# Low parts of the recurrence outputs moved from VectorE to GpSimd, and a new order at the seam between recurrence and attention, in a hybrid decoder block

## The chip, the cores and the metric

The kernel runs on one core of one Trainium2 chip. The metric is the device time of one execution in microseconds; the time of the kernel before is the median of three runs.

## What is computed

One decoder block on 512 tokens plus 16 prepended meta tokens, width 1024, all in float32. The reference, cut to the parts that matter here:

```python
y = _rmsnorm(h, mix_norm_g[l])
z = y @ w_in[l]
hq, hf, hi, hgate, aq, ak, av, ga, gb = jnp.split(z, offsets, axis=-1)
o_hg = _hgrn2(hq, hf, hi, lbs[l])                      # recurrence, 4 heads of 128
o_hg = _rmsnorm(o_hg, hg_norm_g[l]).reshape(B, L, 512) * jax.nn.silu(hgate)
o_at = _swa_sinks(aq, ak, av, attn_sinks[l])           # window attention, 8 query heads, 2 kv heads
g_hg, g_at = sigmoid(ga + b), sigmoid(gb + b)
m = g_hg * (o_hg @ w_branch_hg[l]) + g_at * (o_at @ w_branch_attn[l])
h = h + m @ w_out[l]
h = h + _peer(_rmsnorm(h, ffn_norm_g[l]), ...)         # product-key experts, 16384 rows of u and v
out = _rmsnorm(h, final_norm_g)[:, N_META:]
```

(Shapes and reshapes are shortened here.) The expert part at the end is by far the longest.

## The kernel before

**Split products.** Every large product is made in three passes on TensorE. A float32 tensor x is held as `hi`, a rounded copy, and `lo` = x - `hi`, and x·w is hi·hi + lo·hi + hi·lo (`SPLIT`). ScalarE makes the `hi` parts (a copy into the rounded type) and GpSimd or VectorE the `lo` parts (a subtraction). The weights come as a stream of tiles of 128 x 1024: SyncE loads one of two raw buffers, ScalarE makes `wzhi` (`split_hi`, line 728), GpSimd `wzlo` (`spread_lo`, line 578), and TensorE then runs 24 products of 512 columns with the tile.

**No scheduler.** Each engine has one instruction stream written out by hand; engines meet at semaphores only. What stands behind a waiting instruction on the same engine waits too.

**The stage of the change.** After the projections come the recurrence (four token tiles, `tt` = 0 to 3) and the attention (steps `i` = 0 to 16, one pair of heads and a token tile of 128 in each). Both are chains of small operations, so TensorE fills its time between them with the 384 products of the 16 gate tiles (`gate_products`, line 1806): 24 before the recurrence, 24 in each `tt`, 8 at the seam (`GATES_MID`) and 15 or 16 in each attention step. Behind each gate tile t:

- ScalarE runs `gate_out(t)` when its 24 products are done: it copies the result out of PSUM (line 790) and makes the `hi` part of weight tile t + 2 (line 728), whose buffer tile t has freed.
- GpSimd then makes the `lo` part of tile t + 2 (line 578) and multiplies gate row t by the row norm (`scale_block`, line 589).
- TensorE needs the `lo` part of tile t + 2 before its first product (`w_lo` in `gate_products`).

**Where `gate_out` stands on ScalarE.** In attention step i, gate tiles finished in the first `GATES_SOON` products of the step come at the step's end; those finished later in it come in the next step:

```python
if i:
    for t in gate_blocks_done(gates_before(i - 1) + GATES_SOON, gates_before(i)):
        gate_out(t)
...
for t in gate_blocks_done(gates_before(i), gates_before(i) + GATES_SOON):
    gate_out(t)
```

**An attention step.** TensorE: transposes of step i - 1 (`turn`, line 1922 and 1923), half of the gate products, `scores(i + 1)`, the other half, and after every fourth step `values` (lines 1932 and 1938). VectorE: `logits(i)` (lines 1330, 1333), then, when ScalarE's exponentials (line 856) are there, `normalise(i)`: a reciprocal (line 1340), two scalings of `atp` by a column (line 1343), and a small product into `atpm` (line 1344), whose end releases `turn(i)`. `queries_lo` (line 1282) makes low parts of later queries in six of the steps.

**The recurrence outputs.** For each `tt` ScalarE takes sums of squares (`o_sq`, line 837) and a root (line 841), VectorE scales (`natural`, line 1265, into `o_nat`), TensorE transposes (`turn_outputs`, line 1866), VectorE multiplies with the output gate into `o_hg` (`gated`, line 1274). For the last `tt` this happens at the seam, inside attention step 0. Later ScalarE makes `ohg["hi"]` of one head in steps 2, 4, 6 and 8 (line 899), and VectorE makes `ohg["lo"]` in steps 3, 7, 11 and 14 (`HG_LO`, line 1377). The branch products after the attention need all of them.

Of the kernel before, what the change touches and what calls it, by code (L numbers as in the profile page):

```python
# [118 lines left out]
HD_AT = 2  # L119
QUERY_HI = {3: 2, 7: 3}  # L120
QUERY_LO = {1: (1, 0), 2: (1, 1), 4: (2, 0), 6: (2, 1), 8: (3, 0), 10: (3, 1)}
HG_LO = (3, 7, 11, 14)
GATES_SOON = 8
QUARTERS = 4
SPAN = LEN // 2
XSUM_AT = 6
# [77 lines left out]
def build(nc, xT, x, params, sinks, ffn_g, final_g, wstream, uT, u, v, gates_dram, acc_dram, out):  # L204
    ctx = ExitStack()
    with ctx:
# [340 lines left out]
        def _(pool):  # L547
# [66 lines left out]
                pool.tensor_tensor(key_lo[s][:], key_raw[:, s], key_hi[:, s].bitcast(F32), ALU.subtract  # L614
                                   ).then_inc(S["key_ok"], 1)

            for t in range(2):
                spread_lo(T_GATE + t + 2, t % 2)
                scale_block(gates[:, t:t + 1], "gate_copied", t + 1, "gate_out")
                keys_lo(t)  # L620
            scale_blocks(T_GATE + 2, T_BRANCH - 2, gates, T_GATE, "gate_copied", "gate_out")
            for t in range(N_GATE - 2, N_GATE):
                split_lo(T_GATE + t + 2, t % 2, slot(t % 2))
                scale_block(gates[:, t:t + 1], "gate_copied", t + 1, "gate_out")
# [92 lines left out]
        def _(act):  # L717
# [113 lines left out]
            act.wait_ge(S["z_out"], N_Z)  # L831
            act.activation(osig[:], og_z, ACT.Sigmoid).then_inc(S["og_sig"], 1)
            for tt in range(TT):
                act.wait_ge(S["o_mm"], (tt + 1) * P // CH)
                for r in range(PER):
                    c = tt * PER + r
                    act.activation(o_sq[:, r, :], ps[:, tt % 2, r * P:(r + 1) * P], ACT.Square,
                                   accum_out=o_stat[:, 0, c:c + 1]).then_inc(S["o_sum"], 1)
                own = slice(tt * PER, (tt + 1) * PER)
                act.wait_ge(S["o_sum"], (tt + 1) * PER)  # L840
                act.activation(o_stat[:, 1, own], o_stat[:, 0, own], ACT.Sqrt, bias=eps[:], scale=1.0 / P
                               ).then_inc(S["osd_ok"], 1)
                for t in gate_blocks_done(GATES_TURN + tt * GATES_HG, GATES_TURN + (tt + 1) * GATES_HG):
                    gate_out(t)
                if tt == TT - 2:
                    act.wait_ge(S["wsc_mm"], TT)
                    queries_hi(0)
                    queries_hi(1)
# [291 lines left out]
        def _(dve):  # L1140
# [221 lines left out]
            for i in range(HEADS):  # L1362
                logits(i)
                if i == 0:
                    natural(TT - 1)
                    gated(TT - 1)
                if i and i % 4 == 0:
                    meta_lo(i // 4 - 1)
                normalise(i)
                if i in QUERY_LO:  # L1370
                    queries_lo(*QUERY_LO[i])
                if i >= 5 and i % 4 == 1:
                    attention_lo(i // 4 - 1)
                if i in HG_LO:
                    h = HG_LO.index(i)
                    dve.wait_ge(S["ohg_hi"], h + 1)
                    dve.tensor_tensor(ohg["lo"][:, h, :], o_hg[:, h, :], ohg["hi"][:, h, :].bitcast(F32),
                                      ALU.subtract).then_inc(S["ohg_ok"], 1)
            meta_lo(TT - 1)
            attention_lo(TT - 1)  # L1380

# [319 lines left out]
        def _(pe):  # L1701
# [205 lines left out]
            pe.wait_ge(S["z_out"], N_Z)  # L1907
            scores(0)
            gate_products(GATES_TURN + TT * GATES_HG, GATES_TURN + TT * GATES_HG + GATES_MID)
            turn_outputs(TT - 1)  # L1910

            def turn(p):

                tt, c = p // 4, p % 4
# [26 lines left out]
            for i in range(HEADS + 1):  # L1941
                if i:
                    turn(i - 1)
                first, last = gates_before(i), gates_before(i + 1)
                gate_products(first, (first + last) // 2)
                if i + 1 < HEADS:
                    scores(i + 1)
                gate_products((first + last) // 2, last)
                if i and i % 4 == 0:
                    values(i // 4 - 1)  # L1950
# [373 lines left out]
```

## Time and profile before

| | |
|---|---|
| median of 3 runs | 1558.53 us (1558.51 to 1559.04) |
| profiled execution | 1558.55 us, its span 1556.7 us |
| TensorE matmul | 1548.4 us busy, 99% of the span |
| VectorE | 1280.5 us, 82% |
| GpSimd | 753.8 us, 48% |
| ScalarE | 695.4 us, 45% |
| granted TensorE clock | 1.0 of full speed over the whole span |

The span runs from the first to the last instruction; 1.85 us of the time lie outside it. Recurrence and attention, the stage of the change, lie between 130 and 262.6 us. A busy TensorE in this table can still lose time, since matmuls overlap in the pipeline: inside the stage it is better read from the distance between starts, which is 0.23 us for gate products that follow one another.

### The profile page before, as it was taken

Reading aid. Unit: us, or ns where it says so; the run is one execution under the profiler, and the core shown is the slowest. Engines: PE = TensorE matmul, PEld = TensorE weight load, DVE = VectorE, ACT = ScalarE, POOL = GpSimd, SP = SyncE. Lnnn points to the kernel's source line nnn. Section 1 sums busy time; section 2 is a strip of 40 time slices with the busy share of each in tenths; the row PEclk is TensorE's granted clock in tenths of the full one; section 3 lists DMA queues with packets and bytes.
Section 4 is the critical chain, followed back from the end, with each engine's and each line's share of the span. In section 5 each row is a group of like instructions: output and inputs, shape, how many; then the busy total and the mean of one; then the engine's idle time right before and its main releaser. Section 6 shows DMA issues by size and latency. Waiting matters only on the chain.

```text
span 1556.7 us, 25687 instructions
## 1 busy us (share of the span) xinstructions
PE 1548.4 (99%) x9433; PEld 1377.6 (88%) x9433; DVE 1280.5 (82%) x2548; ACT 695.4 (45%) x1012; POOL 753.8 (48%) x484
## 2 busy tenths in 40 slices
PE   9999999999999999999999999999999999999998
PEld 9987777888889999999989899999999999888887
DVE  5898665836899899999588787888888888888887
ACT  6333566444343477777433333333333333333334
POOL 4675345434566566654255455555545455322220
PEclk9999999999999999999999999999999999999999
DMA  4322122433224489998899999998999989988984
GB/s 163 97 95 75 63 68 89 142 123 135 81 85 146 142 276 320 322 326 264 311 369 359 338 343 344 341 352 337 347 345 341 358 328 333 328 302 318 334 319 147
DMA packets 151730, 385.44 MB, mean 248 GB/s; under 512 B 11872, under 2 KB 61536, under 8 KB 151520
## 3 DMA queue, kind: packets, MB, share of 16 engines
q1 hardware_dynamic: 59328, 203.13, 36.3%
q0 software_dynamic: 41472, 151.01, 27.1%
q10 hardware_dynamic: 50848, 30.30, 6.7%
q8 instruction: 40, 0.66, 0.2%
q14 instruction: 42, 0.34, 0.1%
HBM read 355.03 MB, written 28.84 MB: 247 GB/s over the span
## 4 chain that ended last, share of the span: by engine, by line
PE 83%; DVE 10%; issue 5%; POOL 2%; ACT 1%; ACTq 0%; POOLq 0%
PE ps L2221 32%; PE ps L2064 26%; PE ps L1743 6%; PE ps L2082 5%; PE ps L1970 3%; DVE hot_w L1627 3%; DVE rows L1566 3%; PE ps L1806 1%; PE ps L1983 1%; DVE hot_l L1623 1%; DVE hot_l L1628 1%; DVE hot_l L1624 1%; PE ps L2207 1%; PE ps L2145 1%; PE ps L1751 1%
## 5 line engine op out<-in xcount | busy, mean ns | idle before, releaser
L2064 PE MATMUL ps<-hThi,uwhi 128*128 128x352 f32 x1024 | 330.1, 326 | 0.0
L2064 PE MATMUL ps<-hTlo,uwhi 128*128 128x352 f32 x1024 | 327.7, 322 | 0.0
L1017 ACT ACTIVATE vwhi<-vraw 128x1024 fp32r<-128x1024 f32 x128 | 135.8, 1061 | 408.0 <-PE ps L2221 353.7
L686 POOL DMA_INDIRECT rows<-in_v,gidx x128 | 163.2, 1275 | 251.3 <-DVE acc L1582 235.1
L686 POOL DMA_INDIRECT rows<-in_u,gidx x128 | 189.2, 1478 | 182.3 <-DVE rows L1575 138.5
L1541 DVE TENSOR_TENSOR vwlo<-vraw,vwhi 128x1024 fp32r<-128x1024 f32 x128 | 156.6, 1223 | 112.3 <-ACT vwhi L1017 112.1
L971 ACT ACTIVATE uwhi<-uraw 128x1024 fp32r<-128x1024 f32 x127 | 134.3, 1058 | 168.8 <-PE ps L2064 133.4
L2064 PEld LDWEIGHTS ps<-hTlo,uwhi 128*128 128x128 f32 x1024 | 192.6, 188 | 1.6
L2064 PEld LDWEIGHTS ps<-hThi,uwhi 128*128 128x128 f32 x1024 | 192.2, 188 | 1.9 <-issue 0.3
L2064 PE MATMUL ps<-hThi,uwlo 128*128 128x352 f32 x1024 | 183.8, 322 | 0.0
L2221 PE MATMUL ps<-vwhi,awhi 128*128 128x512 f32 x720 | 183.7, 390 | 0.0
L2221 PE MATMUL ps<-vwlo,awhi 128*128 128x512 f32 x720 | 182.7, 389 | 0.0
L2221 PE MATMUL ps<-vwhi,awlo 128*128 128x512 f32 x720 | 182.7, 389 | 0.0
L646 POOL TENSOR_TENSOR uwlo<-uraw,uwhi 128x1024 fp32r<-128x1024 f32 x52 | 125.4, 2411 | 96.7 <-ACT uwhi L971 63.2
L1582 DVE SCALAR_TENSOR_TENSOR acc<-rows,pick_w,acc 128x1024 f32<-128x1024 f32 x128 | 164.4, 1284 | 4.2 <-DMA rows<-in_v,gidx 1.7
L2064 PEld LDWEIGHTS ps<-hThi,uwlo 128*128 128x128 f32 x1024 | 166.7, 188 | 0.0
L2221 PEld LDWEIGHTS ps<-vwlo,awhi 128*128 128x128 f32 x720 | 135.1, 188 | 28.3
L2221 PEld LDWEIGHTS ps<-vwhi,awlo 128*128 128x128 f32 x720 | 135.2, 188 | 28.1
L1575 DVE SCALAR_TENSOR_TENSOR rows<-rows,ynat 128x1024 f32<-128x1024 f32 x128 | 154.8, 1231 | 6.1 <-DMA rows<-in_u,gidx 6.0
L2221 PEld LDWEIGHTS ps<-vwhi,awhi 128*128 128x128 f32 x720 | 134.0, 188 | 25.7
L578 POOL TENSOR_TENSOR wzlo<-raw,wzhi 128x1024 fp32r<-128x1024 f32 x35 | 86.3, 2467 | 110.4 <-ACT wzhi L728 110.3
L1058 ACT ACTIVATE piece<-ps 128x512 f32<-128x512 f32 x96 | 100.9, 1168 | 16.0 <-PE ps L2145 16.0
(382 smaller groups left out, 2959.3 us busy)
## 6 DMA issues: line engine op xcount, KB each, us to landing
vraw<-in_v SPq DMA_DIRECT2D x128, 512.0 KB, 5.4
uraw<-in_uT SPq DMA_DIRECT2D x127, 512.0 KB, 5.1
raw<-in_wstream SPq DMA_DIRECT2D x70, 512.0 KB, 3.5
gmat<-gates_dram SPq DMA_DIRECT2D x64, 384.0 KB
gates_dram<-piece ACTq DMA_DIRECT2D x11, 2048.0 KB, 14.4
xt<-in_xT SPq DMA_DIRECT2D x8, 264.0 KB, 4.9
acc<-in_x ACTq DMA_DIRECT2D x4, 512.0 KB, 4.5
rows<-in_u,gidx POOLq DMA_INDIRECT x128, 7.3
```

The source lines that it names most:

```text
L578: pool.tensor_tensor(spaced(k, "lo"), loaded(k), spaced(k, "hi").bitcast(F32), ALU.subtract).then_inc(S["w_lo"], 1)
L646: pool.tensor_tensor(u_weights("lo", n, False), uraw[:, n % 2, :], u_weights("hi", n, False).bitcast(F32), ALU.subtract).then_inc(S["u_lo" ...
L686: pool.indirect_dma_start(out=rows[n % SLOTS][:], out_offset=None, in_=u if q < P else v, in_offset=bass.IndirectOffsetOnAxis(ap=gidx[:, q ...
L971: act.activation(u_weights("hi", n, n >= LAG), u_raw(n, k), ACT.Copy).then_inc(S["u_hi"], 1)
L1017: act.activation(vw["hi"][:, m % 2, :], vraw[:, m % 2, :], ACT.Copy).then_inc(S["v_hi"], 1)
L1058: act.activation(piece[o % 2][:, :, t:t + 4].rearrange("p i t -> p t i"), ps[:, 4 + batch % 2 * 2 + q, :].rearrange("p (t i) -> p t i", t= ...
L1541: dve.tensor_tensor(vw["lo"][:, m % 2, :], vraw[:, m % 2, :], vw["hi"][:, m % 2, :].bitcast(F32), ALU.subtract).then_inc(S["v_lo"], 1)
L1575: dve.scalar_tensor_tensor(out=row[:], in0=row[:], scalar=1.0, in1=ynat[:, 0, :], op0=ALU.mult, op1=ALU.mult, accum_out=dots[:, k:k + 1]). ...
L1582: dve.scalar_tensor_tensor(out=acc[:, 0, :], in0=row[:], scalar=pick_w[:, k:k + 1], in1=acc[:, 0, :], op0=ALU.mult, op1=ALU.add).then_inc( ...
L1743: ins = pe.matmul(dst, z_weights(k, a, c), y[b][:, SLOT[c], own], start=i == 0, stop=i == 3 * DC - 1)
L2064: ins = pe.matmul(ps[:, k, 0:UCOLS], u_weights(a, k, far)[:, c * P:(c + 1) * P], hT[b][:, c, P + EXTRA:TOK], start=i == 0, stop=i == len(U ...
L2221: ins = pe.matmul(ps[:, 2 + j, :], act_w[a][:, k, j // 2 * P:(j // 2 + 1) * P], vw[b][:, k, j % 2 * 512:(j % 2 + 1) * 512], start=first an ...
```

## The change

1. `ohg["lo"]` is made by GpSimd, head h right behind `scale_block` of gate tile 7 + h; VectorE no longer makes it. GpSimd's loop over gate tiles is written out for this.
2. `GATES_SOON` goes from 8 to 11. Of the 16 gate tiles this moves `gate_out(6)` from step 3 to the end of step 2, and `gate_out(11)` from step 11 to the end of step 10.
3. At the seam: ScalarE runs `gate_out(4)` ahead of the last sums of squares instead of behind the root; VectorE runs the last `gated` behind `normalise(0)` instead of ahead of it; TensorE runs the last `turn_outputs` behind `scores(1)`, 7 gate products and one pair of score products later.

```diff
-HG_LO = (3, 7, 11, 14)
-GATES_SOON = 8
+HG_LO = (7, 8, 9, 10)
+GATES_SOON = 11
...
-            for t in range(2):
+            for t in range(N_GATE - 2):
                 spread_lo(T_GATE + t + 2, t % 2)
                 scale_block(gates[:, t:t + 1], "gate_copied", t + 1, "gate_out")
-                keys_lo(t)
-            scale_blocks(T_GATE + 2, T_BRANCH - 2, gates, T_GATE, "gate_copied", "gate_out")
+                if t < 2:
+                    keys_lo(t)
+                if t in HG_LO:
+                    h = HG_LO.index(t)
+                    pool.wait_ge(S["ohg_hi"], h + 1)
+                    pool.tensor_tensor(ohg["lo"][:, h, :], o_hg[:, h, :], ohg["hi"][:, h, :].bitcast(F32),
+                                       ALU.subtract).then_inc(S["ohg_ok"], 1)
...
             for tt in range(TT):
+                if tt == TT - 1:
+                    for t in gate_blocks_done(GATES_TURN + tt * GATES_HG, GATES_TURN + (tt + 1) * GATES_HG):
+                        gate_out(t)
                 act.wait_ge(S["o_mm"], (tt + 1) * P // CH)
...
-                for t in gate_blocks_done(GATES_TURN + tt * GATES_HG, GATES_TURN + (tt + 1) * GATES_HG):
-                    gate_out(t)
+                if tt < TT - 1:
+                    for t in gate_blocks_done(GATES_TURN + tt * GATES_HG, GATES_TURN + (tt + 1) * GATES_HG):
+                        gate_out(t)
...
                 if i == 0:
                     natural(TT - 1)
-                    gated(TT - 1)
                 if i and i % 4 == 0:
                     meta_lo(i // 4 - 1)
                 normalise(i)
+                if i == 0:
+                    gated(TT - 1)
...
-                if i in HG_LO:
-                    h = HG_LO.index(i)
-                    dve.wait_ge(S["ohg_hi"], h + 1)
-                    dve.tensor_tensor(ohg["lo"][:, h, :], o_hg[:, h, :], ohg["hi"][:, h, :].bitcast(F32),
-                                      ALU.subtract).then_inc(S["ohg_ok"], 1)
...
             gate_products(GATES_TURN + TT * GATES_HG, GATES_TURN + TT * GATES_HG + GATES_MID)
-            turn_outputs(TT - 1)
...
                 if i + 1 < HEADS:
                     scores(i + 1)
+                if i == 0:
+                    turn_outputs(TT - 1)
                 gate_products((first + last) // 2, last)
```

ScalarE at the seam, before (`gates<-ps` and the `wzhi` behind it are one `gate_out`; the second is that of tile 4):

```order
L825 ACTIVATE query<-zr 64x512 x4
L837 ACTIVATE o_sq,o_stat<-ps 128x128 x4
L841 ACTIVATE o_stat<-o_stat,eps 128x4
L790 ACTIVATE gates<-ps 128x512
L728 ACTIVATE wzhi<-raw 128x2x512
L856 ACT_TABLE_LOAD
L856 ACTIVATE atp,atstat<-atsc,atstat 128x145 x4
```

and with the change:

```order
L830 ACTIVATE query<-zr 64x512 x4
L795 ACTIVATE gates<-ps 128x512
L733 ACTIVATE wzhi<-raw 128x2x512
L845 ACTIVATE o_sq,o_stat<-ps 128x128 x4
L849 ACTIVATE o_stat<-o_stat,eps 128x4
L865 ACT_TABLE_LOAD
L865 ACTIVATE atp,atstat<-atsc,atstat 128x145 x4
```

`gate_out(4)` has moved from behind the root to ahead of the squares.

ScalarE in attention steps 2 and 3, before:

```order
L856 ACTIVATE atp,atstat<-atsc,atstat 128x145 x2
L864 ACTIVATE atpT<-ps 128x2x128
L899 ACTIVATE ohghi<-o_hg 128x512
L856 ACTIVATE atp,atstat<-atsc,atstat 128x145 x2
L864 ACTIVATE atpT<-ps 128x2x128
L790 ACTIVATE gates<-ps 128x512
L728 ACTIVATE wzhi<-raw 128x2x512
L825 ACTIVATE query<-zr 64x512 x2
```

and with the change:

```order
L865 ACTIVATE atp,atstat<-atsc,atstat 128x145 x2
L873 ACTIVATE atpT<-ps 128x2x128
L795 ACTIVATE gates<-ps 128x512
L733 ACTIVATE wzhi<-raw 128x2x512
L908 ACTIVATE ohghi<-o_hg 128x512
L865 ACTIVATE atp,atstat<-atsc,atstat 128x145 x2
L873 ACTIVATE atpT<-ps 128x2x128
L830 ACTIVATE query<-zr 64x512 x2
```

`gate_out(6)` now stands ahead of the exponentials of step 3 and of the first head's `ohghi`.

GpSimd around gate tiles 6 to 8, with the change (before, it is the same pair `wzlo`, `gates` in a loop, with nothing between the pairs):

```order
L578 TENSOR_TENSOR wzlo<-raw,wzhi 128x2x512
L589 TENSOR_TENSOR gates<-gates,rstd 128x512
L578 TENSOR_TENSOR wzlo<-raw,wzhi 128x2x512
L589 TENSOR_TENSOR gates<-gates,rstd 128x512
L625 TENSOR_TENSOR ohglo<-o_hg,ohghi 128x512
L578 TENSOR_TENSOR wzlo<-raw,wzhi 128x2x512
L589 TENSOR_TENSOR gates<-gates,rstd 128x512
L625 TENSOR_TENSOR ohglo<-o_hg,ohghi 128x512
```

Three subtractions or products now follow one another on GpSimd in four places where there were two.

## Rows read from the trace of the kernel before

**Rows 1.** The page: span, and busy time of each engine.
```profile
span 1556.7 us, 25687 instructions
PE 1548.4 (99%) x9433; PEld 1377.6 (88%) x9433; DVE 1280.5 (82%) x2548; ACT 695.4 (45%) x1012; POOL 753.8 (48%) x484
```

**Rows 2.** Timeline of TensorE at the seam: start us, us, engine, line, operation [idle, releaser].
```profile
177.88 0.39 PE L1806 MATMUL ps<-ylo,wzhi 128*128 128x512 f32 x1
178.44 0.66 PE L1866 MATMUL ps<-ident,o_nat 128*128 128x128 f32 x4 [0.17 <-DVE o_nat L1265]
...
182.62 0.39 PE L1806 MATMUL ps<-ylo,wzhi 128*128 128x512 f32 x1
183.06 0.44 PE L1922 MATMUL ps<-ident,atp 128*128 128x128 f32 x2
```

**Rows 3.** Timeline of TensorE, starts of gate tiles 8, 10, 13; turns 7 and 10.
```profile
196.93 0.40 PE L1806 MATMUL ps<-yhi,wzlo 128*128 128x512 f32 x1
197.29 0.50 PE L1806 MATMUL ps<-yhi,wzhi 128*128 128x512 f32 x1
...
213.56 0.40 PE L1806 MATMUL ps<-yhi,wzhi 128*128 128x512 f32 x1
...
215.42 0.60 PE L1922 MATMUL ps<-ident,atp 128*128 128x128 f32 x4
...
231.18 0.60 PE L1922 MATMUL ps<-ident,atp 128*128 128x128 f32 x4
...
236.95 0.40 PE L1806 MATMUL ps<-yhi,wzlo 128*128 128x512 f32 x1
237.80 0.50 PE L1806 MATMUL ps<-yhi,wzhi 128*128 128x512 f32 x1 [0.45 <-POOL wzlo L578]
```

**Rows 4.** Timeline of ScalarE at the seam: first square, then the copy and split of tile 4.
```profile
175.85 0.28 ACT L837 ACTIVATE o_sq<-ps 128x128 f32<-128x128 f32 x1 [4.05 <-PE ps L1857]
...
177.35 0.58 ACT L790 ACTIVATE gates<-ps 128x512 f32<-128x512 f32 x1
177.83 1.05 ACT L728 ACTIVATE wzhi<-raw 128x1024 fp32r<-128x1024 f32 x1
```

**Rows 5.** Timeline of GpSimd, steps 2, 5 and 7 and the first branch tile.
```profile
186.58 2.40 POOL L578 TENSOR_TENSOR wzlo<-raw,wzhi 128x1024 fp32r<-128x1024 f32 x1 [3.95 <-ACT wzhi L728]
188.94 1.29 POOL L589 TENSOR_TENSOR gates<-gates,rstd 128x512 f32 x1
...
203.16 1.30 POOL L589 TENSOR_TENSOR gates<-gates,rstd 128x512 f32 x1
...
212.46 1.31 POOL L589 TENSOR_TENSOR gates<-gates,rstd 128x512 f32 x1
...
269.73 2.41 POOL L574 TENSOR_TENSOR wlo<-raw,whi 128x1024 fp32r<-128x1024 f32 x1 [1.19 <-ACT whi L726]
```

**Rows 6.** Timeline of VectorE: `normalise` in steps 1 and 2, and a sum beside the branches.
```profile
185.03 0.48 DVE L1343 TENSOR_SCALAR atp<-atp,atstat 128x128 f32<-128x128 f32 x2
...
188.48 1.83 DVE L1343 TENSOR_SCALAR atp<-atp,atstat 128x128 f32<-128x128 f32 x2
190.23 0.18 DVE L1344 TENSOR_TENSOR atpm<-atp,atstat 128x32 f32<-128x32 f32 x1
...
269.86 2.82 DVE L1391 TENSOR_TENSOR mtmp<-mtmp 128x512 f32<-128x512 f32 x1
```

**Rows 7.** The same, `normalise` in steps 5, 7 and 10.
```profile
203.86 1.01 DVE L1343 TENSOR_SCALAR atp<-atp,atstat 128x256 f32<-128x256 f32 x2
...
212.69 1.49 DVE L1343 TENSOR_SCALAR atp<-atp,atstat 128x256 f32<-128x256 f32 x2
214.10 0.18 DVE L1344 TENSOR_TENSOR atpm<-atp,atstat 128x32 f32<-128x32 f32 x1
...
229.80 0.18 DVE L1344 TENSOR_TENSOR atpm<-atp,atstat 128x32 f32<-128x32 f32 x1
```

**Rows 8.** Line 1377: durations ns min/median/max, first and last start us.
```profile
L1377 DVE TENSOR_TENSOR ohglo<-o_hg,ohghi x4: 679/682/686, 193.8 to 249.8; 128x512 fp32r<-128x512 f32 x4
```

## The prediction

> **What bounds the kernel now.** I read the page first, then the stage's timelines, engine by engine. On the page TensorE is busy for 1548.4 of 1556.7 us [rows 1]: the kernel is bound by its matmuls, and a change that takes none away can win only time in which TensorE stands still. No matmul goes here. So the question is how long TensorE stands still between 130 and 262.6 us, and whether other work makes it wait where it did not.
>
> Its timeline there shows starts 0.23 us apart for gate products in a row, and a transpose 0.24 us behind a product where nothing is waited for. Against these, four places are late:
> - the last `turn_outputs` starts 0.56 us behind the product ahead of it, named releaser `o_nat` [rows 2]: 0.32 us lost;
> - `turn(0)` starts 0.44 us behind its product [rows 2]: 0.20 us lost;
> - gate tile 8 starts 0.36 us behind tile 7 and its first product takes 0.50 instead of 0.40 us [rows 3]: 0.24 us lost;
> - gate tile 13 starts 0.85 us behind tile 12, released by GpSimd's `wzlo` [rows 3]: 0.62 and 0.11, 0.73 us lost.
>
> That is 1.49 us, 0.1% of the time, and all that this change can win in the stage. Changes within 0.2% (3.1 us) are what a measurement of this kernel can't tell from none.
>
> **Part by part: the seam.** ScalarE's squares began at 175.85 and its root was over when the copy of tile 4 began at 177.35; that `gate_out` costs 1.5 us [rows 4]. It now runs first, and can: the 24 products of tile 4 end at about 175.2. So squares begin about 1.0 us later, at 176.85, the root ends at 178.4 and `o_nat` at about 179.35. TensorE wants it now behind 8 + 7 gate products and `scores(1)`, at about 180.1 instead of 178.2: 0.75 us of slack, and the 0.32 us go. The exponentials of step 0 come about 0.5 us earlier, as `gate_out(4)` no longer stands ahead of them, `normalise(0)` no longer waits for `gated`, and tile 6's `wzlo` and the `gates` product on GpSimd are over before it. `turn(0)` is then released at about 181.6 and reached at 182.5: the 0.20 us go. Seam: **-0.52 us**.
>
> **`GATES_SOON`.** `gate_out(6)` can run when tile 6 is done, at about 190.1, inside an idle stretch of ScalarE; `wzlo` of tile 8 is then over at 194.1, well ahead of 197.3: **-0.24 us**. In the same way `gate_out(11)` runs at 230.6, and `wzlo` of tile 13 ends near 235 where 237.8 was needed: **-0.73 us**. Nothing else on ScalarE is lengthened; `ohghi` and the exponentials of step 3 come 0.8 us later behind it.
>
> **The subtraction on GpSimd.** VectorE loses four operations of 0.68 us [rows 8]. They cost nothing before: each stood behind the `normalise` that releases a turn, and no turn was waiting. So they win nothing directly. On GpSimd one takes about 1.3 us, as the `gates` product of the same 512 columns does [rows 5]; GpSimd has the time, since each of its pairs was followed by over 1.8 us of idle.
>
> What it costs is the other engine's time. `normalise` has two scalings that take 0.48 us together with GpSimd idle, and took 1.83 us in step 2, where GpSimd went from `wzlo` to `gates` at 188.94 [rows 5, 6]. The first waited for the end of `wzlo`; the second for the end of `gates` at 190.23, and `atpm` came then. A GpSimd operation right behind another thus holds back the next VectorE operation that works from SBUF, and I take this for `ohglo` too. The sum on VectorE at 269.86 took 2.82 us beside GpSimd's 2.41 [rows 5, 6], so operations with two SBUF inputs wait as well.
>
> The Trainium skill, "SBUF — State Buffer", section "SBUF: two separate sides", says that VectorE and GpSimd share one pair of SBUF ports under an exclusive lock: the one that started keeps it for its whole instruction, against VectorE operations in a 2-port mode or with two SBUF inputs. The trace agrees, 1.83 against 0.48 us. By that rule `queries_lo` in step 10, with two SBUF inputs, would wait for a whole `wzlo` of 2.4 us if it came second; then the sum below would be about 2 us larger. I take it to come first, by half a microsecond.
>
> Now the four places. `ohglo` 0 follows `gates` of tile 7, which ended at 204.46 beside `normalise(5)`: its first scaling began at 203.86 and the pair took 1.01 us [rows 5, 7]. The second now waits until about 205.7, and `normalise(5)` ends some 1.0 us later; TensorE comes for it with 1.4 us in hand. But the loop of VectorE and ScalarE (logits, exponentials, `normalise`) has no slack up to step 7, so some 0.6 us of it (0.4 are absorbed by the earlier start) arrive there, and `gates` of tile 8 moves with it. In step 7 the pair already took 1.49 us beside `gates` (212.46 to 213.77), and `atpm` ended at 214.28, 1.14 us ahead of `turn(7)` at 215.42 [rows 3, 5, 7]. With 0.6 us of delay `gates` ends at 214.35, `ohglo` 1 at 215.65, `atpm` at 215.85. TensorE, 0.56 us earlier by then (0.52 + 0.24 less 0.2 of step 3 below) and 0.15 later again, comes at 215.0. It waits: **+0.85 us**. The 0.15 us are gate tile 10, whose `wzlo` moves from 212.5 to 213.1 while TensorE would come at 213.0 instead of 213.56 [rows 3]: **+0.15 us**.
>
> `ohglo` 2 meets the `normalise` behind `values(1)`, with 1.5 us of slack: nothing. `ohglo` 3 meets `normalise(10)`, whose `atpm` ended at 229.98, 1.2 us ahead of the turn at 231.18 [rows 3, 7]; with 1.3 us added and step 9's delay of 0.5 I get 0.4 us for `turn(10)` and, as the earlier `wzlo` and `gates` of tile 11 now stand in `normalise(11)`, 0.4 us for `turn(11)`: **+0.8 us** (bounds 0 and 2.6, two whole operations of 1.3). In step 3 the earlier pair of tile 6 stands beside `normalise(3)`: between 0 and 1.3 us, I take **+0.2 us**, near the low end, since its turn has the most slack of these.
>
> Sum: -1.49 + 0.85 + 0.15 + 0.8 + 0.2 = **+0.5 us** on the profiled 1558.55, which is at the median of 1558.53: **1559.0 us**. Nothing behind 262.6 us changes but its start; the last `ohglo` is ready earlier than before.
>
> **Rivals.**
> - *The stalls go and nothing takes their place*: the turns' slack of 1.1 us and more absorbs every meeting. For it: VectorE is 2.7 us lighter. Against it: step 7 had 1.14 us and gets 1.3 plus a delay. Time: 1558.5 - 1.5 = 1557.0.
> - *GpSimd takes the chain of the turns* and each `ohglo` delays TensorE by its full length: 4 x 1.3 - 1.5 = +3.7, so 1562.2, slower. This decides if the delay of one meeting is still there at the next, so that no slack is left in any of the four. For it: the loop has no slack between steps 5 and 7. Against it: ScalarE and VectorE wait for TensorE's `values` after every fourth step, which restores the slack. The rule of the shared ports in the Trainium skill, the same page, is what would bring this about.
> - *The change doesn't do what it says*: `gate_out(6)` and `(11)` wait on ScalarE for their 24 products, and the exponentials behind them are late by what the tiles gain. Against it: in both steps ScalarE stood idle when the 24 products were done. Time: 1558.55 - 0.5 + 0.2, about 1558.3.
>
> **How the numbers follow.** Forecast 0.44, first rival 0.33, third 0.11, slower rival 0.07; 0.05 is left for something in the long stages behind, 0.03 of it faster and 0.02 slower. Forecast and first and third rival lie within 0.2%, and what the unknown meetings can add (up to 2.4 us over my sum) reaches 1561.4, still within it; 0.01 of the forecast's chance lies above. That makes 0.10 for slower by over 0.2%. Faster by that much would need more idle TensorE time than the stage has: 0.03. The rest, 0.87, is within 0.2%. Range: from just below the first rival, 1556.8, to 1561.4.
>
> **What would show it.** Right: TensorE's starts at the seam and at tiles 8 and 13 0.23 us apart; two-scaling groups of `normalise` near 1.6 us or more in steps 5, 7 and 10 with `ohglo` of 1.3 us beside them; `turn(7)` late by 0.5 us or more; span 1557.2. Wrong: all turns on time (first rival), or branch products beginning later than 264 instead of 262.67 (the slower one). It would also be wrong in its ground if the time moved by more than 2 us while the branch products started within 1 us of before: then something outside the stage decides.

## The result, and the profile after

| | before | with the change |
|---|---|---|
| median of 12 runs each, on the same chip | 1558.88 us | 1563.73 us |
| lowest to highest | 1558.51 to 1561.51 | 1561.29 to 1565.32 |
| ratio, with its 95% interval | | 1.003 [1.0022, 1.0037] |
| profiled execution | 1558.55 us | 1563.12 us |

The change makes the kernel slower by 0.3%. The forecast was 1559.0 us, with a range up to 1561.4: the time lies above the range, and on the side that had a chance of 0.10.

The page of the kernel after, its first part, beside [rows 1]:

```profile
span 1561.3 us, 25638 instructions
PE 1550.2 (99%) x9433; PEld 1379.0 (88%) x9433; DVE 1281.7 (82%) x2544; ACT 695.6 (45%) x1012; POOL 758.4 (49%) x488
```

GpSimd has four instructions and 4.6 us more. VectorE has four fewer, but its busy time did not fall by 4 x 0.68 us: it rose by 1.2 us. The page hides a part of this: the stages behind, which are the same in both programs, differ by over 3 us of VectorE's busy time between the two executions. In the stage of the change alone VectorE is busy for 95.9 us instead of 91.2, with four instructions fewer, since an instruction that is held back counts as busy. TensorE's busy time is 1.8 us longer with the same 9433 matmuls; half of that is explained below.

**Where the time went.** Both programs run the same matmuls in nearly the same order, so I compared when each of them starts, less 0.12 us by which this trace is behind at the start of the stage. "Late" means later than before; each place is read at a matmul in it or right behind it.

| place | late by, us | step from the place ahead | the prediction's term |
|---|---|---|---|
| `turn(0)`, the seam behind it | -0.64 | -0.64 | -0.52 |
| `turn(3)` | -0.45 | +0.19 | +0.2 |
| gate tile 8 | -0.62 | -0.17 | -0.24 |
| gate tile 10 | -0.24 | +0.38 | +0.15 |
| `turn(7)` | +0.65 | +0.89 | +0.85 |
| `turn(10)` | +1.48 | +0.83 | +0.8, with `turn(11)` |
| `scores(12)` | +3.71 | **+2.23** | none |
| `turn(11)` | +5.36 | **+1.65** | none |
| behind gate tile 13 | +4.63 | -0.73 | -0.73 |
| first branch product, and the last product | +4.61, +4.51 | 0, -0.1 | 0 |

The terms that the prediction had come to +0.75 us instead of +0.5. The other 3.9 us come in one step of the loop, step 10, and in the 4 us behind it. The row of `turn(3)` is read at the start of the turn, which shows only a part of what it cost: TensorE is at -0.72 just ahead of `turn(3)` and at -0.39 right behind it, so that step 3 costs 0.33 us and tile 8 gives 0.23. From the branches on hardly anything changes, as expected. (In the other profiles below, the stages behind the branches drift by up to 0.9 us either way, so an effect of less than a microsecond shows in the stage only, and not in the time.)

First the places that it had. TensorE's timeline in the profile after (start us, us, engine, line, operation, tiles, [idle, releaser]), beside [rows 2, 3]:

```profile
182.54 0.38 PE L1925 MATMUL ps<-ident,atp 128*128 128x128 f32 x2
...
196.67 0.39 PE L1811 MATMUL ps<-yhi,wzlo 128*128 128x512 f32 x1
196.90 0.40 PE L1811 MATMUL ps<-yhi,wzhi 128*128 128x512 f32 x1
...
212.95 0.29 PE L1907 MATMUL ps<-key_lo,query 128*128 128x272 f32 x1
213.34 0.50 PE L1811 MATMUL ps<-yhi,wzhi 128*128 128x512 f32 x1
...
215.07 0.39 PE L1811 MATMUL ps<-ylo,wzhi 128*128 128x512 f32 x1
216.14 0.65 PE L1925 MATMUL ps<-ident,atp 128*128 128x128 f32 x4 [0.68 <-DVE atpm L1353]
...
231.79 0.40 PE L1811 MATMUL ps<-ylo,wzhi 128*128 128x512 f32 x1
232.72 0.66 PE L1925 MATMUL ps<-ident,atp 128*128 128x128 f32 x4 [0.53 <-DVE atpm L1353]
```

`turn(0)` starts at 182.54 instead of 183.06. Tile 8 starts 0.23 us behind tile 7: its stall is gone. Tile 10 now starts 0.39 us behind a product of the scores, where 0.13 was the pace, so it waits where it did not. `turn(7)` starts 1.07 us behind its product instead of 0.24, and `turn(10)` 0.93 instead of 0.24, both released by `atpm`.

What `turn(7)` and `turn(10)` lose is not all that the chain of VectorE and ScalarE loses. In step 8 the third subtraction, `ohglo` 2, stands beside `normalise(8)`. VectorE before, then VectorE and GpSimd with the change:

```profile
219.47 0.62 DVE L1343 TENSOR_SCALAR atp<-atp,atstat 128x256 f32<-128x256 f32 x2
```

```profile
220.25 1.74 DVE L1352 TENSOR_SCALAR atp<-atp,atstat 128x256 f32<-128x256 f32 x2
```

```profile
220.26 1.32 POOL L625 TENSOR_TENSOR ohglo<-o_hg,ohghi 128x512 fp32r<-128x512 f32 x1
```

The pair of scalings is longer by 1.1 us. `turn(8)` has the slack for it, and TensorE loses nothing there. But VectorE's own chain has none: `normalise(9)` and `normalise(10)` both begin 1.5 us later than before, the offset of the traces taken off.

And now the place that it did not have. TensorE some 2 us further on:

```profile
234.72 0.39 PE L1811 MATMUL ps<-yhi,wzlo 128*128 128x512 f32 x1
237.19 0.42 PE L1906 MATMUL ps<-key_hi,query 128*128 128x272 f32 x1 [2.08 <-DVE atstat L1342]
...
238.08 0.63 PE L1811 MATMUL ps<-yhi,wzhi 128*128 128x512 f32 x1
238.51 0.63 PE L1811 MATMUL ps<-ylo,wzhi 128*128 128x512 f32 x1
...
240.64 0.48 PE L1811 MATMUL ps<-yhi,wzhi 128*128 128x512 f32 x1
240.97 0.39 PE L1811 MATMUL ps<-ylo,wzhi 128*128 128x512 f32 x1
```

`scores(12)` waits 2.08 us, and behind it gate products start 0.43 us apart instead of 0.23. The release came from `atstat`, the row maximum of `logits(11)` on VectorE. VectorE's timeline shows what made that late:

```profile
229.81 2.76 DVE L1352 TENSOR_SCALAR atp<-atp,atstat 128x256 f32<-128x256 f32 x2
232.49 0.18 DVE L1353 TENSOR_TENSOR atpm<-atp,atstat 128x32 f32<-128x32 f32 x1
232.70 2.92 DVE L1291 TENSOR_TENSOR query<-zr,query 64x512 fp32r<-64x512 f32 x1
235.65 0.72 DVE L1339 SCALAR_TENSOR_TENSOR atsc<-ps,bandmask 128x544 f32<-128x544 f32 x1
236.41 0.72 DVE L1342 TENSOR_REDUCE atstat<-atsc 128x2 f32<-128x546 f32 x1
```

GpSimd's, in the same stretch:

```profile
229.83 1.28 POOL L589 TENSOR_TENSOR gates<-gates,rstd 128x512 f32<-128x512 f32 x1
231.07 1.35 POOL L625 TENSOR_TENSOR ohglo<-o_hg,ohghi 128x512 fp32r<-128x512 f32 x1
232.68 2.39 POOL L578 TENSOR_TENSOR wzlo<-raw,wzhi 128x1024 fp32r<-128x1024 f32 x1 [0.27 <-ACT wzhi L733]
```

The two timelines interlock. The first scaling of `normalise(10)` ends within 0.2 us of `gates`, the second within 0.2 us of `ohglo` 3 (232.42), and the short `atpm` slips through at 232.49. Then both engines reach for the next operation in the same instant: GpSimd's `wzlo` of gate tile 13 starts 0.016 us ahead of VectorE's `queries_lo` (232.683 and 232.699 in the trace), and `queries_lo` takes 2.92 us instead of the 0.69 us that it took before, when GpSimd was idle there. By the Trainium skill, "SBUF — State Buffer", section "SBUF: two separate sides", whichever of the two starts first holds the shared ports for its whole instruction; the trace agrees, 2.92 us beside a `wzlo` of 2.39.

`logits(11)` stand behind `queries_lo` on VectorE, and `scores(12)` is released by the last of them.

The table of windows, after: us, then busy time (and instructions) of each engine, granted clock, DMA share, GB/s.

```profile
234.00:238.00 4.00, 1.92 (x9) 1.38 (x8) 3.07 (x3) 0.83 (x3) 2.75 (x2) 0.93 0.44 123
238.00:242.00 4.00, 4.00 (x17) 3.23 (x16) 2.24 (x6) 0.83 (x4) 0.00 (x0) 0.65 0.04 12
242.00:246.00 4.00, 4.00 (x20) 3.11 (x18) 2.28 (x7) 3.96 (x9) 0.00 (x0) 1.00 0.00 0
```

Mean granted clocks of 0.93 and 0.65 say that TensorE ran part of both windows at the lower of its two levels, 1.2 GHz; (0.07 + 0.35) x 4 us of clock are missing, 1.7 us, which at half speed is 3.4 us of time. Finer windows put these between 237.4 and 240.8, so the fall came just behind the start of `scores(12)`. Ahead of the fall TensorE had stood still three times: for 0.68 us at `turn(7)`, for 0.53 at `turn(10)`, and for 2.08 at `scores(12)`. The Trainium skill, "TensorE: Matmul & The Clock Gate", section "Back-to-back issue gap", gives a product's spacing at the lower level as its columns divided by 1.2, in ns; for 512 columns that is an estimate of 427. The trace agrees, 430. Matmuls at half the clock also count as busy for longer: that is half of the 1.8 us on the page (the second profile of the change, below, in which the clock did not fall, has 1549.3 us).

### The profile page after: what moved, and what is told of

Read it like the earlier page. It is cut to its first block, busy times and chain, and to the rows that moved or that the text cites. A ratio compares the mean times of both kernels' runs of the same rounds, so it can differ in the third digit from the quotient of the medians.

```text
span 1561.3 us, 25638 instructions
## 1 busy us (share of the span) xinstructions
PE 1550.2 (99%) x9433; PEld 1379.0 (88%) x9433; DVE 1281.7 (82%) x2544; ACT 695.6 (45%) x1012; POOL 758.4 (49%) x488
## 4 chain that ended last, share of the span: by engine, by line
PE 86%; DVE 11%; ACT 1%; issue 1%; DMA 0%; ACTq 0%; POOL 0%; SPq 0%
PE ps L2226 31%; PE ps L2069 26%; PE ps L1748 6%; PE ps L2087 5%; PE ps L1811 4%; PE ps L1975 3%; DVE hot_w L1632 3%; DVE rows L1571 2%; PE ps L1988 1%; DVE hot_l L1628 1%; DVE hot_l L1633 1%; DVE hot_l L1629 1%; PE ps L2212 1%; PE ps L2150 1%; PE ps L1756 1%; PE ps L1710 1%
```

## The experiments

Two theories stood behind the first four kernels. **Theory A**: most of the loss is one lost race in step 10, `queries_lo` against `wzlo` of tile 13, with the fall of the clock that follows it; without it the change costs about what the prediction's terms say. **Theory B**: every meeting of GpSimd with VectorE costs, the delays of the turns add up, and step 10 is only where it shows. "Late" is TensorE's delay against before at the first branch product, read as in the table above. All ratios are against the kernel before on the same chip; the four sets of experiments ran on four chips, so a time is compared with its own kernel before first.

### The race alone

`query_first` makes GpSimd wait for `queries_lo` before this one `wzlo`, and alters nothing else of the change:

```diff
             for t in range(N_GATE - 2):
+                if t == 11:
+                    pool.wait_ge(S["query_ok"], 2 * TT)
```

> The change with one wait more: GpSimd's wzlo behind gate tile 11 waits until the last queries_lo (step 10) is done. Nothing else moves. Theory A (a race for the SBUF ports in step 10: wzlo started 0.02 us ahead of queries_lo, which then took 2.92 instead of 0.69 us, scores(12) waited 2.1 us and TensorE ran at half clock for 3.4 us behind it): queries_lo back at 0.69 us, no wait at scores(12), clock 1.0 throughout, about 3.5 us faster than the change, 1560.2 us. Theory B (every meeting of ohglo with normalise costs a turn, and step 10 is only the sum of them): within 1 us of the change, 1563.7 us, or slower by the added wait.

Measured: 1560.18 us (1559.65 to 1561.88), ratio 1.0006 [0.9997, 1.0015], late by 1.19 us. VectorE and GpSimd in the profile of `query_first`, step 10:

```profile
232.60 0.18 DVE L1355 TENSOR_TENSOR atpm<-atp,atstat 128x32 f32<-128x32 f32 x1
232.81 0.69 DVE L1293 TENSOR_TENSOR query<-zr,query 64x512 fp32r<-64x512 f32 x1
```

```profile
233.57 2.40 POOL L578 TENSOR_TENSOR wzlo<-raw,wzhi 128x1024 fp32r<-128x1024 f32 x1 [1.05 <-DVE query L1293]
```

`queries_lo` is back at 0.69 us, `scores(12)` is on time, and the granted clock is 1.00 through the stage. A `wzlo` that starts about 0.8 us later takes 3.4 of the 4.6 us away: theory A, and with the size that it gave. The turns' delays are all still there (late by 0.66 at `turn(7)`, by 1.49 at `turn(10)`), and `turn(11)` adds 0.43.

`query_step9` takes the same operation out of the race in another way, one step earlier:

```diff
-QUERY_LO = {1: (1, 0), 2: (1, 1), 4: (2, 0), 6: (2, 1), 8: (3, 0), 10: (3, 1)}
+QUERY_LO = {1: (1, 0), 2: (1, 1), 4: (2, 0), 6: (2, 1), 8: (3, 0), 9: (3, 1)}
```

> The change with the last queries_lo in step 9 instead of step 10. Theory A: no VectorE operation with two SBUF inputs stands where wzlo behind gate tile 11 starts, except atpm; scores(12) on time, 3 to 4 us faster than the change, about 1560.2 us. Theory B: the same time within 1 us.

Measured: 1559.44 us (1559.05 to 1561.02), ratio 1.0003 [0.9994, 1.0012], late by 0.75 us. The second way gives the same answer. `turn(10)` loses its 0.8 us here too, so that loss does not hang on where `queries_lo` stands.

`query_behind` does the opposite. Three small writes of zeros stand ahead of `queries_lo` on VectorE, so that it comes second for certain:

```diff
+                if i == 10:
+                    for _ in range(3):
+                        chain.done(dve.memset(rowstat[:, 2, :], 0.0))
                 if i in QUERY_LO:
```

> The change with three small fills of an unused column on VectorE ahead of queries_lo in step 10, so that it comes some 0.3 to 0.4 us behind wzlo instead of 0.02 us. Theory A: wzlo always has the ports first; queries_lo ends when wzlo ends as in the change, so the profile is that of the change and the median about that of the change (1562 to 1564 us), but no run is near 1559 to 1560 us, if those of the change are runs in which queries_lo came first. If such runs are as frequent as in the change (5 of 12 in the second series), something else makes them.

Measured: 1563.2 us (1561.12 to 1565.32, 10 runs), ratio 1.0026 [1.0016, 1.0035]; the profiled execution took 1561.12, late by 3.02 us. Its step 10, VectorE, then GpSimd:

```profile
232.38 0.33 DVE L1382 MEMSET rowstat<- 128x4 f32 x3
232.75 2.60 DVE L1291 TENSOR_TENSOR query<-zr,query 64x512 fp32r<-64x512 f32 x1
```

```profile
232.41 2.40 POOL L578 TENSOR_TENSOR wzlo<-raw,wzhi 128x1024 fp32r<-128x1024 f32 x1 [0.22 <-ACT wzhi L733]
```

The granted clock stayed at 1.00 in this profile, behind waits of 0.70, 0.58 and 2.04 us. No run is below 1561.1 here. Against `query_first`, where the race is won for certain, this is 1.8 us more at the branches in the profiles, and 2.8 us in the medians, each less the median of its own kernel before.

### The change once more

`change_again` is the change, unaltered, in another set of runs.

> The change itself once more. Theory A: the port goes to wzlo again in step 10, scores(12) waits about 2.1 us, and the granted clock is at half for about 3.4 us behind it, which costs about 1.6 us; 1563.7 us. If the order of the two operations, 0.02 us apart, were a matter of luck, a profile with queries_lo at 0.69 us and about 1560 us would come up.

Measured: 1561.94 us, 12 runs from 1558.87 to 1564.86, ratio 1.0018 [1.0008, 1.0027]. Five of the twelve runs lie between 1558.9 and 1560.6, four between 1564.1 and 1564.9, three between. The profiled execution took 1562.46 and was late by 3.17 us at the branches. In it:

```profile
233.06 2.93 DVE L1291 TENSOR_TENSOR query<-zr,query 64x512 fp32r<-64x512 f32 x1
```

```profile
233.05 2.39 POOL L578 TENSOR_TENSOR wzlo<-raw,wzhi 128x1024 fp32r<-128x1024 f32 x1 [0.27 <-ACT wzhi L733]
```

```profile
237.56 0.39 PE L1906 MATMUL ps<-key_hi,query 128*128 128x272 f32 x1 [2.09 <-DVE atstat L1342]
...
238.17 0.39 PE L1811 MATMUL ps<-yhi,wzhi 128*128 128x512 f32 x1
238.40 0.39 PE L1811 MATMUL ps<-ylo,wzhi 128*128 128x512 f32 x1
```

The race was lost again, by 0.012 us, and `scores(12)` waited the same 2.09 us. But the products behind it are 0.23 us apart: the clock did not fall. From `scores(12)` to the turn behind its eight gate products it is 2.47 us here (237.56 to 240.03) and 4.01 us in the first profile (237.19 to 241.20). So the fall of the clock is worth 1.54 of the 1.65 us in the table; the remaining 0.11 us is the first score product, issued 0.23 instead of 0.12 us ahead of the next in both.

So the profiles show two outcomes of one kernel: the race lost with the clock falling, 1563.12, and lost without, 1562.46. A third, the race won, stands in no profiled execution of the change. That the five runs under 1561 us are those is supported, not shown: `query_first`, where it is always won, has a median of 1560.18, and `query_behind`, where it is always lost, has no run that low.

The mean granted clock that is listed with each run, to three digits, says something on how often the clock fell. It is 0.998 in 6 of the 12 first runs of the change, in 2 of the 12 of `change_again` and in 5 of the 10 of `query_behind`; in the 110 runs of the other ten kernels of this document it never is, and in 110 runs of the kernel before it is once, in one of 1564.05 us. So the fall comes with the long wait at `scores(12)` but is not bound to it, and not every long run has it: the longest of `query_behind`, 1565.32 us, is listed with 0.999.

### One part of the change at a time

`seam_only` is the kernel before with the seam's new order alone (the code of the change, without the other two parts).

> The kernel before with the seam's new order alone (gate_out(4) ahead of the squares, gated behind normalise(0), turn_outputs behind scores(1)). The prediction's term: 0.52 us faster than before, starts of the seam's transposes 0.24 us behind their products. If the seam is what costs (rival), at or above the time before.

Measured: 1558.09 us (1556.26 to 1559.01), ratio 0.9993 [0.9984, 1.0002], early by 1.05 us. The seam gives -0.72 up to `turn(3)`, and tile 8's stall of 0.25 us disappears with it: `wzlo` of tile 8 comes 1.1 us earlier and TensorE only 0.7, so it is early enough without `GATES_SOON`. Twice the expected 0.52.

`soon_only` is the kernel before with one number altered:

```diff
-GATES_SOON = 8
+GATES_SOON = 11
```

> The kernel before with GATES_SOON = 11 alone. Prediction's terms: -0.24 - 0.73 + 0.2 = 0.8 us faster than before, no wait at scores(12), as queries_lo of step 10 comes about 1.3 us ahead of wzlo. If the earlier wzlo is a cost by itself, slower than before by 1 us or more.

Measured: 1558.11 us (1557.46 to 1559.58), ratio 0.9998 [0.9989, 1.0007], early by 0.45 us. Tile 13's stall goes (-0.73), tile 8's too (-0.18), but `turn(3)` costs +0.33 and `turn(11)` +0.18: the earlier pairs of `wzlo` and `gates` stand beside these steps' `normalise`, as the prediction had it, and eat half of the gain.

`seam_and_soon` has both, with the four subtractions left on VectorE in the steps where they were:

```diff
-HG_LO = (7, 8, 9, 10)
+HG_LO = (3, 7, 11, 14)
...
+                if i in HG_LO:
+                    h = HG_LO.index(i)
+                    dve.wait_ge(S["ohg_hi"], h + 1)
+                    dve.tensor_tensor(ohg["lo"][:, h, :], o_hg[:, h, :], ohg["hi"][:, h, :].bitcast(F32),
+                                      ALU.subtract).then_inc(S["ohg_ok"], 1)
```

> The change with ohg lo left on VectorE in steps 3, 7, 11 and 14. Theory A and the prediction's terms: -0.5 (seam), -0.24 and -0.73 (gate tiles 8 and 13), +0.2 (step 3): 1.3 us faster than before, about 1557.7 us, and the best version of all. If the earlier wzlo of gate tile 11 meets queries_lo without ohglo too, then as slow as the change, 1563 us.

Measured: 1558.09 us (1557.17 to 1559.79), ratio 0.9996 [0.9987, 1.0005], early by 1.08 us. The whole loss of the change, and 1 us more, goes when the subtractions go back to VectorE. In this kernel `wzlo` of tile 13 stands just as early as in the change; what is missing is the `ohglo` ahead of it.

`lows_only` is the third part alone: the subtractions on GpSimd, with the seam and `GATES_SOON` as before.

> The kernel before with ohg lo on GpSimd alone (behind gate tiles 7 to 10; GATES_SOON = 8, seam as before). Theory A: no race in step 10; turn(7) and turn(10) late by some tenths each, tile 13's stall kept: about 1 us slower than before, at most 2. Theory B (the subtractions on GpSimd are the whole loss): 4 to 5 us slower.

Measured: 1561.59 us (1560.91 to 1563.51), ratio 1.0018 [1.0009, 1.0027], late by 2.87 us. That is more than the 2 us that were to be the most. `turn(7)` gives +0.89 and `turn(10)` +0.84, as in the change, tile 10 +0.16, and there is no race (`wzlo` of tile 13 comes at 238.17, long after `queries_lo`). The surprise is tile 13, in TensorE's timeline of `lows_only`, beside 0.45 us in [rows 3]:

```profile
238.74 0.40 PE L1806 MATMUL ps<-yhi,wzlo 128*128 128x512 f32 x1
240.58 0.50 PE L1806 MATMUL ps<-yhi,wzhi 128*128 128x512 f32 x1 [1.45 <-POOL wzlo L578]
```

With `GATES_SOON` at 8, `gate_out(11)` stands on ScalarE behind the exponentials of step 11, and these wait for VectorE's late logits. So the delay of the turns reaches tile 13, whose stall grows by 1.0 us. In the change that place is cured by `gate_out(11)` moving ahead of the exponentials, and this very move brings `wzlo` under `queries_lo`.

`change_soon8` shows the same from the other side. It is the change with that one number back:

```diff
-GATES_SOON = 11
+GATES_SOON = 8
```

> The change with GATES_SOON back at 8, so that wzlo behind gate tile 11 comes in step 11 again. Theory A: no race in step 10, so 3.9 us less; the stalls at gate tiles 8 and 13 come back (+0.24 and +0.73 us) and the one of step 3 goes (-0.2 us): about 3.1 us faster than the change, 1560.6 us, 1.7 us slower than before. Theory B: only the stalls at the tiles change, about +0.8 us, 1564.5 us.

Measured: 1561.25 us (1560.52 to 1562.14), ratio 1.0015 [1.0005, 1.0024], late by 2.22 us. No race and no fall of the clock, but tile 13's stall larger by 1.0 us, which I had not put into the expectation. Theory A holds for what the race costs, and is too simple on the rest: the turns' delays are a second loss that comes out at tile 13 when the race is taken away in this manner. That is the part of theory B that is right.

### Other places for the subtractions

`head3_late` moves only the last of the four, from behind tile 10 to behind tile 12:

```diff
-HG_LO = (7, 8, 9, 10)
+HG_LO = (7, 8, 9, 12)
```

> The change with the fourth ohglo behind gate tile 12 instead of 10 (HG_LO = 7, 8, 9, 12). Theory A: normalise(10) is no longer held back by it, queries_lo comes 1.3 us ahead of wzlo, turn(10) is on time (-0.8 us) and scores(12) too (-3.9 us): 1559.0 us. Theory B: one of four meetings moved, the same time within 1 us, 1563.7 us.

Measured: 1559.34 us (1558.3 to 1560.73), ratio 1.0002 [0.9993, 1.0011], late by 0.55 us. VectorE in step 10 of `head3_late`, then GpSimd:

```profile
229.28 1.72 DVE L1352 TENSOR_SCALAR atp<-atp,atstat 128x256 f32<-128x256 f32 x2
230.93 0.18 DVE L1353 TENSOR_TENSOR atpm<-atp,atstat 128x32 f32<-128x32 f32 x1
231.14 0.69 DVE L1291 TENSOR_TENSOR query<-zr,query 64x512 fp32r<-64x512 f32 x1
```

```profile
232.16 2.41 POOL L578 TENSOR_TENSOR wzlo<-raw,wzhi 128x1024 fp32r<-128x1024 f32 x1 [1.57 <-ACT wzhi L733]
```

The pair of scalings takes 1.72 us, not 2.76; `turn(10)` is on time, and `queries_lo` is 1.0 us ahead of `wzlo`. This one subtraction, behind tile 10, is what cost `turn(10)` its 0.8 us and set up the race. `turn(11)` then loses 0.4 us, but not to this subtraction: it runs only at 245.07, long behind that turn, and `normalise(11)` stands beside the earlier `wzlo` and `gates` as in `query_first`, which loses the same 0.4. The only loss behind the new place is 0.12 us at gate tile 15.

`lows_free` puts all four where the loop seemed to have most slack, the last two behind tiles 13 and 14:

```diff
-HG_LO = (7, 8, 9, 10)
+HG_LO = (9, 12, 13, 14)
```

> The change with its four ohglo on GpSimd behind gate tiles 9, 12, 13 and 14 instead of 7 to 10. Theory A: there the turns have more slack than the 1.3 us that an operation takes (tile 9 cost none in the change), so TensorE waits for none of them, and only the gains and the 0.2 us of step 3 stay: branch products begin about 1.1 us earlier than before, about 1557.8 us. Theory B (each subtraction on GpSimd costs wherever it stands): 1 us or more slower than before.

Measured: 1559.12 us (1558.26 to 1560.22), ratio 1.0000 [0.9991, 1.0008], neither late nor early. It was 0.95 us early behind tile 13 and lost that 16 us later, 0.2 at gate tile 15 and the rest at `turn(15)`. VectorE, GpSimd and TensorE in the profile of `lows_free`:

```profile
253.04 2.11 DVE L1357 TENSOR_SCALAR atp<-atp,atstat 128x256 f32<-128x256 f32 x2
255.07 1.28 DVE L1358 TENSOR_TENSOR atpm<-atp,atstat 128x32 f32<-128x32 f32 x1
```

```profile
253.66 1.34 POOL L589 TENSOR_TENSOR gates<-gates,rstd 128x512 f32<-128x512 f32 x1
254.96 1.35 POOL L625 TENSOR_TENSOR ohglo<-o_hg,ohghi 128x512 fp32r<-128x512 f32 x1
```

```profile
255.46 0.39 PE L1816 MATMUL ps<-ylo,wzhi 128*128 128x512 f32 x1
256.41 0.66 PE L1930 MATMUL ps<-ident,atp 128*128 128x128 f32 x4 [0.56 <-DVE atpm L1358]
```

Here it is `atpm` that is held back: 32 columns, 1.28 us instead of 0.18. I had expected a gain of over 1 us from my reading of the slack. It did not come.

### The version that is left

`seam_tile11` is the kernel before with the seam and with only `gate_out(11)` moved ahead (tile 8 needs no help once the seam is done, and `turn(3)` keeps its cover); no subtraction moves.

```diff
+            def soon(i):
+                return 11 if i == 10 else GATES_SOON
...
-                    for t in gate_blocks_done(gates_before(i - 1) + GATES_SOON, gates_before(i)):
+                    for t in gate_blocks_done(gates_before(i - 1) + soon(i - 1), gates_before(i)):
...
-                for t in gate_blocks_done(gates_before(i), gates_before(i) + GATES_SOON):
+                for t in gate_blocks_done(gates_before(i), gates_before(i) + soon(i)):
```

> The kernel before with the seam's new order, and of the two moved gate_out only that of tile 11 (ohg lo stays on VectorE). Sum of what the single parts showed: -1.0 us at the seam and tile 8, -0.7 us at tile 13, no wait at turn(3): branch products begin 1.7 us earlier than before, 1557.2 us, the best version.

Measured: 1557.48 us (1556.16 to 1559.31), ratio 0.9991 [0.9982, 1.0000], early by 1.50 us, the lowest time of all. Tile 13 in its profile:

```profile
236.25 0.39 PE L1814 MATMUL ps<-yhi,wzlo 128*128 128x512 f32 x1
236.48 0.40 PE L1814 MATMUL ps<-yhi,wzhi 128*128 128x512 f32 x1
```

It starts 0.23 us behind tile 12, and what is left of loss is `turn(11)` with 0.18 us. The interval ends at 1.0000, so as a time this is a gain only just; as a difference between the two traces it is clear.

## Why the prediction was wrong

Point by point, by its own steps:

- **What bounds the kernel.** Right. The four late places are the ones there were, and `seam_tile11` wins 1.50 us net where 1.49 were counted (the seam gave 0.2 more, `turn(11)` took 0.18, so that the close match is chance).
- **The seam, -0.52.** Right in sign and mechanism; -0.64 at `turn(0)` and -0.72 just ahead of `turn(3)`. Alone it also removes tile 8's stall, -1.05 in all (`seam_only`), which I had credited to `GATES_SOON`.
- **`GATES_SOON`, -0.24 and -0.73.** Right: -0.23 and -0.73.
- **Step 3, +0.2.** Right in mechanism, a little small: +0.33, and +0.33 in `soon_only`, where it has no other cause.
- **`turn(7)`, +0.85, and tile 10, +0.15.** The first right: +0.89. The second came to +0.38.
- **`turn(10)` and `turn(11)`, +0.8 together.** +0.83, but all of it at `turn(10)`; I had given it 0.4. `turn(11)` had nothing left to lose, since TensorE was already late by more than its `normalise`; where TensorE comes on time, it costs 0.2 to 0.4 us (`seam_and_soon`, `head3_late`). The sum was right by luck.
- **"`ohglo` 2 meets the `normalise` behind `values(1)`, with 1.5 us of slack: nothing."** True for `turn(8)`, and wrong for the chain. The pair of scalings took 1.1 us longer, and this was still there at `normalise(10)`: 1.5 us of delay, where the prediction reckoned with "step 9's delay of 0.5".
- **GpSimd's time.** "Each of its pairs was followed by over 1.8 us of idle" holds behind gate tiles 7 to 10, where the subtractions went. Behind three other pairs of the loop it is 1.62 to 1.78 us.
- **"I take it to come first, by half a microsecond."** This is the step that failed, and the term above is why. The sentence named the right pair, `queries_lo` and `wzlo` in step 10, and the price, "about 2 us larger". It then took one side of a comparison of two late times. Without the subtractions on GpSimd (`seam_and_soon`) `queries_lo` starts 1.82 us ahead of this `wzlo`. In the change `queries_lo` starts 3.10 us later than there, 2.08 from the later `normalise(10)` and 1.02 from its longer pair of scalings, and `wzlo`, which follows TensorE's delay, 1.26 us later. The lead comes to nothing: the measured order was the other one, by 0.016 us, and `scores(12)` lost 2.23 us. A lead of half a microsecond between two engines that both hang on chains of estimated delays should have been a rival with a chance of its own, not a choice.
- **The clock.** This is the term that was left out. No step of the prediction asked what a wait of TensorE does to the clock. It added 1.54 us in the profiled execution and nothing in the second one.
- **The range.** The other order at its price gives 1559.0 + 2.2 = 1561.2, which the range up to 1561.4 still held; without the fall of the clock the profiled execution would have been at about 1561.6 (an estimate, 1563.12 - 1.54), just above it. So the wait, with the 0.25 us by which the other terms were too low, reaches the edge of the range, and the clock carries the time clear of it. The range was also drawn narrower than the prediction's own bounds: 2.6 for the late turns and 1.3 for step 3 allow 2.9 us over the sum, not 2.4.
- **The slower rival**, "GpSimd takes the chain of the turns and each `ohglo` delays TensorE by its full length": wrong as a mechanism. The turns that follow a subtraction lost 0.89 + 0.83 us, far from 4 x 1.3, and the first and third `ohglo` cost TensorE nothing at their turns. The sign that the prediction gave for it came all the same, branch products later than 264 (they begin at 267.4), by way of the race and the clock. Its condition, "if the delay of one meeting is still there at the next", did hold for VectorE between steps 5 and 7 and between steps 8 and 10, and it is what brought `queries_lo` into the race. The other two rivals fall: the stalls went but others took their place, and ScalarE did run the moved copies early.

**The cause in one sentence, as the runs show it:** the last subtraction behind tile 10 holds back `normalise(10)` on top of a chain that the one before it has already made late, and `GATES_SOON` = 11 puts the next `wzlo` at that very moment; take away either (`seam_and_soon`, `change_soon8`, `head3_late`), or order the two (`query_first`, `query_step9`), and the wait at `scores(12)` is gone.

This holds for the wait of 2.2 us. The fall of the clock, 1.54 us more, followed it in one of three profiled executions that had the wait (the change, `change_again`, `query_behind`). What stays open: why the clock fell in one execution and not in the others, with the same waits ahead of it; and which runs of the change are those where `queries_lo` came first.

## What to carry to other kernels

Moving an elementwise operation from VectorE to GpSimd did not free VectorE here, where it landed directly behind another GpSimd operation: count, at each landing place, the next VectorE operations that work from SBUF, and charge them the length of the GpSimd one. Where two engines reach for the same resource within a microsecond and each comes there through delays that were estimated, give both orders a chance and price the bad one; if one order is much cheaper, fix it with a wait. And try the parts of a change apart: two of these three win 1.1 us together, and the third loses 5.7 on top of them, 1.5 of which are the clock's in that one execution.

## What was not expected of the hardware

- A lead of 0.016 us (0.012 in the second profile) was enough for `wzlo` to hold back `queries_lo`, with a wait of 2.2 us behind it. No profile shows what a lead as small does the other way round. The same program ran between 1558.87 and 1564.86 us in one sequence of 12, where the kernel with the order fixed (`query_first`, on another chip) stayed between 1559.65 and 1561.88.
- The size of the held-back operation did not matter here: `atpm` with 32 columns waited 1.28 us in `lows_free`, and got through at once in the change (0.18 us, between `ohglo` and `wzlo`). What the two have different is whether GpSimd was inside an operation at that moment.
- It works in the other direction as well: `gates` behind `wzlo`, started while `queries_lo` was ending, took 1.72 us instead of 1.28 to 1.30:

```profile
235.03 1.72 POOL L589 TENSOR_TENSOR gates<-gates,rstd 128x512 f32<-128x512 f32 x1
```

- TensorE's granted clock fell to 1.2 GHz after the waits of 0.68, 0.53 and 2.08 us in one profiled execution, and stayed at 2.4 GHz after 0.67, 0.53 and 2.09 us in another of the same program. The table of windows of `change_again`, at the place where the change's first profile had 0.93 and 0.65:

```profile
234.00:238.00 4.00, 1.91 (x10) 1.30 (x9) 3.44 (x3) 0.46 (x2) 3.12 (x2) 1.00 0.35 97
238.00:242.00 4.00, 4.00 (x23) 3.33 (x22) 2.24 (x6) 2.37 (x8) 0.00 (x0) 1.00 0.10 38
```
